# End of a two-layer streaming encoder: output rows of two token groups formed token-major from the old X and the last Y

## The chip, the cores and the metric

The kernel runs on one core of a Trainium2 chip. The metric is device time in microseconds. The engines are named as the profile names them: PE is TensorE (PEld its weight loads), DVE is VectorE, ACT is ScalarE, POOL is GpSimd, SP is SyncE. SP only issues loads and stores here.

## What is computed

One inference step of a two-layer encoder over 512 new prompt tokens and 32 sample tokens, with 1024 features each. Only the end of each layer matters here:

```python
def _rms(x, g):
    y = x32 * lax.rsqrt(jnp.mean(x32 * x32, axis=-1, keepdims=True) + EPS) * g
...
    f = jnp.square(jax.nn.relu(_rms(x, p['g_mlp_pre']) @ p['w_up'])) @ p['w_down']
    x = x + _rms(f, p['g_mlp_post'])
```

After the last layer, `x` is the output `y_prompt` (512 by 1024) and `y_sample` (32 by 1024). The norm needs the sum of squares of `f` over all 1024 features of a token before any feature of that token can be finished.

## The kernel before, in words

All activations lie feature-major in the on-chip memory: 128 features on the partitions, 8 blocks of features (k or m = 0 to 7), 544 tokens on the free axis. `X` holds x, `Y` holds f. A projection takes a weight tile of 128x1024 numbers (512 KB), which ACT splits into a high part (L1136) and DVE into a low part (L1611); PE runs three products for each of 8 blocks and two halves of the tokens.

The 544 tokens are cut in two ways. `HC` halves them: half 0 is tokens 0 to 287, half 1 is tokens 288 to 543. `cols(grp)` names five groups for the turning at the end: group 0 (the 32 sample tokens), groups 1 and 2 (prompt tokens in half 0), groups 3 and 4 (half 1, 128 tokens each).

The end of the last layer runs so:

- `down_four` and `down_end` on PE are the down projections, two output blocks m per round of four weight tiles. The last output block, m = 7, is done in two token halves (L710), half 0 first.
- DVE's `f_tile` and `f_last` add both parts of an output block in `Y` and scale it (L1921, L1925, L1711, L1718). ACT's `f_square` writes its squares and multiplies `Y` by the gain (L1219, L1220). DVE's `y_sum` adds the squares into `acc_y` (L1632).
- `y_half_sum` (L715) multiplies `acc_y` by a matrix of ones, which gives every partition the sum over the features. ACT's `y_rs_half` turns it into the inverse norm `rn` with Ln (L1161) and Exp (L1166).
- DVE's `x_chunk` runs five times for each half: `Y` times `rn` (L1643), then `X` plus `Y` (L1646). The order on DVE is half 0, with the finish of block 7 of half 1 between its chunks, then half 1.
- PE then turns each group of the new `X` to token-major in two sets of four 128x128 transposes (L1126), ACT (L1603) or for groups 3 and 4 also DVE (L2209) evicts each set of 128x512 into `y_out`, and SP stores a group once both its halves are there, in the order 0 to 4 (L521). Two of the banks are used twice, by groups that wait on an eviction.
- Beside it PE turns the last recurrent states (L1114), ACT evicts them as `last_t` (L1597), and POOL stores them in eight small transfers (L670).

The order of the work on every engine is written out by hand; semaphores hold the engines together.

Of the kernel before, what the change touches and what calls it, by code (L numbers as in the profile page):

```python
# [92 lines left out]
def hybrid_encoder(nc, A, out):  # L93
    DEPTH = A["w_in"].shape[0]
    with ExitStack() as ctx:
# [25 lines left out]
        def sem(name):  # L121
# [18 lines left out]
        neg_lam = sb("neg_lam", [P, 2])  # L140
        eps_col = sb("eps_col", [P, 1])
        warm = sb("warm", [P, 1])
        rs_tok = sb("rs_tok", [P, 5])
        mx = sb("mx", [P, 2, 4])
        neg_mx = sb("neg_mx", [P, 2, 4])
# [61 lines left out]
        lsc = at("lsc", [P, 8, KT * 2], F32, BIG + 7 * 4096 + 256)  # L207
        gain_row = at("gain_row", [KT, P], F32, BIG + 7 * 4096 + 1024)
        y_out = at("y_out", [P, 5, 2, 512], F32, BIG)
        last_t = at("last_t", [P, P], F32, BIG + 5 * 4096)  # L210


# [15 lines left out]
            sem, ("h_hi_ready", "h_lo_ready", "x_squared", "x_summed", "x_ssq", "x_rs"))  # L228
        y_squared, y_summed, y_ssq, y_rs, y_scaled, x_new = map(
            sem, ("y_squared", "y_summed", "y_ssq", "y_rs", "y_scaled", "x_new"))  # L230
        half_done, half_evacuated, first_halves_out, xsq_ready, xsq_added = map(
            sem, ("half_done", "half_evacuated", "first_halves_out", "xsq_ready", "xsq_added"))
        rs_turned, rs_tok_ready = sem("rs_turned"), sem("rs_tok_ready")
# [17 lines left out]
        relu2_done, u_hi_ready, u_lo_ready, f_scaled = map(sem, ("relu2_done", "u_hi_ready", "u_lo_ready", "f_scaled"))  # L251
        f_gained, half_trio = sem("f_gained"), sem("half_trio")
        out_turned, last_turned, last_placed, out_stored = map(sem, ("out_turned", "last_turned", "last_placed", "out_stored"))
        out_placed, out_placed_dve = sem("out_placed"), sem("out_placed_dve")
        last_stored = sem("last_stored")

        def own_wait(eng):
# [3 lines left out]

        def out_bank(grp, half):

            if grp in (1, 2):
                return PX[:, 2, :] if (grp, half) == (1, 0) else PJ[:, 1, 0, :] if (grp, half) == (1, 1) else PX[:, 3 * half, :]
            if grp == 3:
                return PX[:, 1, :] if half == 0 else PJ[:, 1, 1, :]
            return PJ[:, 0, half, :]

        def raw(n):  # L270

# [41 lines left out]
        def x_count(S):  # L313

            return 10 * (S - 1)
# [133 lines left out]
        @block.sync  # L449
        def _(sp):  # L450
            def load_x(g):

                if g == 0:
                    sp.dma_start(x_in[0:NS, 0, :], A["x_sample"][0]).then_inc(x_landed[0], 16)
                else:
                    sp.dma_start(x_in[:, g, :], A["x_prompt"][0, P * (g - 1):P * g, :]).then_inc(x_landed[g], 16)

            def load(n, source):

                sp.wait_ge(tile_done, n.value - WR + 1)  # L460
                sp.dma_start(raw(n), source).then_inc(w_landed[n.slot], 16)

            def load_early(n, source):

                need(sp, tile_done, n.value - 2 * WR + 1)
                sp.dma_start(raw(n), source).then_inc(w_landed[n.slot], 16)

            def load_apart(n, source):

                sp.dma_start(raw(n), source).then_inc(w_landed[n.slot], 16)  # L470

            def load_layer(l):

                def pair(p, first=0):
                    for j in range(first, 12):
                        load(TileNo(TL * l + 12 * p + j, j % WR), pair_source(l, p, j))

                pair(0, WR + 1)
                with sp.Fori(1, 4) as p:
                    pair(p)  # L480
                for first, name, block in ((T_GB, "w_in", 48), (T_WA, "w_branch_attn", 0), (T_WL, "w_branch_lru", 0), (T_WO, "w_out", 0)):
                    with sp.Fori(0, KT // WR) as r:
                        for j in range(WR):
                            load(TileNo(TL * l + first + WR * r + j, j), columns(name, l, block + WR * r + j))
                sp.wait_ge(lru_step, 12 * 8 * (l + 1))
                load_apart(mlp_tile(l, 0, 0, 0), columns("w_up", l, 0))
                load_early(mlp_tile(l, 0, 4, 0), columns("w_up", l, 4))
                for j in range(1, WR):
                    load(mlp_tile(l, 0, 0, j), columns("w_up", l, j))
                for j in range(1, WR):  # L490
                    load(mlp_tile(l, 0, 4, j), columns("w_up", l, 4 + j))
                for c in range(2):
                    with sp.Fori(0 if c else 2, 4) as r:
                        for j in range(WR):
                            load(mlp_tile(l, c, 4 * r, j), columns("w_up", l, 16 * c + 4 * r + j))
                    with sp.Fori(0, 4) as r:
                        for j in range(WR):
                            load(mlp_tile(l, c, 16 + 4 * r, j), down_source(l, c, j % 2, 2 * r + j // 2))


            for g in range(3):
                load_x(g)
            for i in range(WR + 1):
                load_apart(pair_tile(0, 0, i), pair_source(0, 0, i))
                if i == 1:
                    load_x(3)
                    load_x(4)
            for l in range(DEPTH):
                load_layer(l)
                if l < DEPTH - 1:  # L510
                    sp.wait_ge(x_ssq, 3 * l + 3)
                    load_apart(pair_tile(l + 1, 0, 0), pair_source(l + 1, 0, 0))
                    load_early(pair_tile(l + 1, 0, WR), pair_source(l + 1, 0, WR))
                    for i in range(1, WR):
                        load(pair_tile(l + 1, 0, i), pair_source(l + 1, 0, i))

            for g in range(5):
                sp.wait_ge(out_placed, 2 * g + 2 if g < 3 else g + 4)
                need(sp, out_placed_dve, g - 2)
                to = out["y_sample"][0] if g == 0 else out["y_prompt"][0, P * (g - 1):P * g, :]  # L520
                sp.dma_start(to, y_out[0:NS if g == 0 else P, g, :, :].rearrange("p a b -> p (a b)")).then_inc(out_stored, 16)  # L521
            sp.wait_ge(out_stored, 16 * 5)
# [152 lines left out]
        def _(pe):  # L675
# [139 lines left out]
            def gates(l, p, u):  # L815
# [6 lines left out]
                        mm = pe.matmul(PX[:, 2 * j + half, 0:LH], w_gate[:, u, j, :], uc[:, LH * half:LH * half + LH], start=True, stop=True)  # L822
                mm.then_inc(gates_done, 1)

            def sub_ssq(l, p, u):
                g2 = 2 * (4 * l + p) + u
                pe.wait_ge(o_squared, g2 + 1)
                pe.wait_ge(lru_act, 5 * g2 + 2)
                ones_sum(sq_o, 2).then_inc(o_ssq, 1)
# [179 lines left out]
            for l in range(DEPTH):  # L1009
# [89 lines left out]
                for c in range(2):  # L1099
# [4 lines left out]
                    if c == 0:  # L1104
                        pe.wait_ge(x_summed, 7 * l + 7)
                        ones_sum(acc_x).then_inc(x_ssq, 1)
                    down_four(l, c, 0)
                    with pe.Fori(1, 4 if c == 0 else 3) as r:
                        down_four(l, c, r)
                down_end(l)  # L1110

            y_half_sum(DEPTH - 1, 1, 1)
            pe.wait_ge(lru_step, 12 * 8 * DEPTH)
            pe.transpose(PX[:, 3, 0:P], last[:].rearrange("p l r k -> p (l r k)"), ident[:]).then_inc(last_turned, 1)  # L1114
            for grp in range(5):
                for half in range(2):

                    pe.wait_ge(x_new, x_count(2 * DEPTH) + 5 * (grp > 2) + 3 + 2 * half)
                    if grp == 2 and half == 1:
                        pe.wait_ge(last_placed, 1)  # L1120
                    if grp == 3 and half == 0:
                        pe.wait_ge(y_rs, 4 * 2 * DEPTH)
                    if grp == 4:
                        pe.wait_ge(out_placed, half + 1)
                    for k in range(4):
                        mm = pe.transpose(out_bank(grp, half)[:, P * k:P * k + P], X[:, 4 * half + k, cols(grp)], ident[:])  # L1126
                    mm.then_inc(out_turned, 1)
# [3 lines left out]
        def _(act):  # L1131
# [223 lines left out]
            def sub_square(l, p, u):  # L1355
# [2 lines left out]
                need(act, o_ssq, g2, first=p + u == 0)  # L1358
                act.activation(sq_o[:], O[:, 2 * p + u, :], ACT.Square).then_inc(o_squared, 1)

            def sub_log(l, p, u):
                g2 = 2 * (4 * l + p) + u
                act.wait_ge(o_ssq, g2 + 1)
# [91 lines left out]
            for l in range(DEPTH):  # L1455
# [118 lines left out]
                for c in range(2):  # L1574
# [11 lines left out]
                    else:  # L1586
                        for r in range(3):
                            down_four(l, c, r)
                down_end(l)
                if l < DEPTH - 1:  # L1590
                    renew(l, 1)
                else:
                    y_rs_half(l, 1, 0)
                    f_square(l, 7, 1)
                    y_rs_half(l, 1, 1)
            act.wait_ge(last_turned, 1)
            act.activation(last_t[:], PX[:, 3, 0:P], ACT.Copy).then_inc(last_placed, 1)  # L1597

            for grp in range(5):
                nr = NS if grp == 0 else P  # L1600
                for half in range(2 if grp < 3 else 1):
                    act.wait_ge(out_turned, 2 * grp + half + 1)
                    act.activation(y_out[0:nr, grp, half, :], out_bank(grp, half)[0:nr, :], ACT.Copy).then_inc(out_placed, 1)  # L1603

# [2 lines left out]
        def _(dve):  # L1607
# [591 lines left out]
            for c in range(5):  # L2199
# [2 lines left out]
                    f_last(DEPTH - 1, 1)  # L2202
                if c == 2:
                    y_sum(DEPTH - 1, 1, 8, HC[1])
            for c in range(5):
                x_chunk(DEPTH - 1, 1, 1, c)
            for grp in range(3, 5):
                dve.wait_ge(out_turned, 2 * grp + 2)
                dve.tensor_copy(y_out[:, grp, 1, :], out_bank(grp, 1)).then_inc(out_placed_dve, 1)  # L2209


# [27 lines left out]
```

## Time and profile before

| what | us |
|---|---|
| median of 3 runs | 2019.92 |
| lowest and highest of them | 2018.5 and 2025.07 |
| the profiled execution, its own time | 2020.43 |
| its span in the trace | 2018.6 |
| PE busy in it | 1975.9 (98%) |
| DVE busy | 1072.3 (53%) |
| ACT busy | 955.6 (47%) |

The profiled execution took 1.8 us more than its span; that part lies around the traced work. It is 0.5 us above the median of the runs. Times of trace rows are counted from the start of the span.

### The profile page before, as it was taken

To read this page: it belongs to the slowest core of one execution; us is meant where nothing else is said; L and a number is where in the kernel's file an instruction comes from. 1 tells how busy PE (TensorE), PEld (TensorE's weight loads), DVE (VectorE), ACT (ScalarE), POOL (GpSimd) and SP (SyncE) were. 2 spreads that over 40 slices of the span, in tenths; PEclk is the share of its full clock that TensorE was granted. 3 is DMA by queue.
4 is the path that set the end of the run, shared out by engine and by line. 5 is a ranking of instruction groups with operands and counts; after the bars stand their busy time and mean duration, and the time that the engine had idled before them with its cause. 6 is when DMAs were issued, how large, how long until landed. Compare 5 with 4: busy or idle time off the path is not lost.

```text
span 2018.6 us, 38666 instructions
## 1 busy us (share of the span) xinstructions
PE 1975.9 (98%) x15630; PEld 1929.2 (96%) x15630; DVE 1072.3 (53%) x1986; ACT 955.6 (47%) x1503; POOL 279.1 (14%) x306
## 2 busy tenths in 40 slices
PE   7999999999999999999989999999999999999997
PEld 7999999999998999999989999999999999999997
DVE  6657575765437432333467676767644464224334
ACT  5466666565236431342365757565732554213333
POOL 4312121100101200120041212120001012002100
PEclk9999999999999999999999999999999999999999
DMA  5323232322332323232323232322223323233331
GB/s 136 107 60 105 63 100 69 83 71 78 93 95 70 87 84 93 84 94 84 98 60 98 64 100 72 99 76 75 74 84 94 95 65 92 84 92 86 90 88 67
DMA packets 308455, 172.00 MB, mean 85 GB/s; under 512 B 7592, under 2 KB 303872, under 8 KB 308320
## 3 DMA queue, kind: packets, MB, share of 16 engines
q1 hardware_dynamic: 300768, 155.47, 27.0%
q0 software_dynamic: 7520, 14.59, 2.6%
q8 instruction: 97, 1.59, 0.3%
q14 instruction: 38, 0.31, 0.1%
q10 hardware_dynamic: 32, 0.04, 0.0%
HBM read 158.86 MB, written 11.21 MB: 84 GB/s over the span
## 4 chain that ended last, share of the span: by engine, by line
PE 81%; ACT 9%; DVE 6%; issue 3%; DMA 1%; SPq 0%; ACTq 0%; DVEq 0%
PE PJ L698 65%; PE PJ L710 3%; PE PJ L880 3%; PE PX L908 2%; ACT w_hi L1136 2%; PE PX L926 1%; DVE w_lo L1611 1%; PE PX L946 1%; DVE T L1722 1%; PE PX L962 1%; PE PX L710 1%; DMA w_raw<-in_w_in 1%; DVE uc L1855 1%; ACT L1353 1%; DVE Y L1643 1%
## 5 line engine op out<-in xcount | busy, mean ns | idle before, releaser
L1611 DVE TENSOR_TENSOR w_lo<-w_raw,w_hi 128x1024 fp32r<-128x1024 f32 x284 | 384.2, 1356 | 371.5 <-ACT w_hi L1136 370.4
L698 PE MATMUL PJ<-h_hi,w_hi 128*128 128x272 f32 x2304 | 489.9, 294 | 2.6 <-DVE T L1722 1.9
L698 PE MATMUL PJ<-h_hi,w_lo 128*128 128x272 f32 x2304 | 474.8, 288 | 0.0
L698 PE MATMUL PJ<-h_lo,w_hi 128*128 128x272 f32 x2304 | 473.8, 287 | 0.0
L1136 ACT ACTIVATE w_hi<-w_raw 128x1024 fp32r<-128x1024 f32 x284 | 297.6, 1051 | 233.4 <-DMA w_raw<-in_w_down 116.9
L698 PEld LDWEIGHTS PJ<-h_hi,w_hi 128*128 128x128 f32 x2304 | 359.3, 189 | 12.8 <-issue 9.5
L698 PEld LDWEIGHTS PJ<-h_lo,w_hi 128*128 128x128 f32 x2304 | 360.7, 188 | 0.0
L698 PEld LDWEIGHTS PJ<-h_hi,w_lo 128*128 128x128 f32 x2304 | 359.5, 189 | 0.0
L698 PE MATMUL PJ<-u_hi,w_hi 128*128 128x272 f32 x960 | 198.4, 288 | 0.0
L698 PE MATMUL PJ<-u_hi,w_lo 128*128 128x272 f32 x960 | 197.4, 288 | 0.0
L698 PE MATMUL PJ<-u_lo,w_hi 128*128 128x272 f32 x960 | 197.1, 287 | 0.0
L659 POOL TENSOR_TENSOR u_lo<-T,u_hi 128x544 f32 x64 | 87.8, 1373 | 595.6 <-ACT u_hi L1386 595.6
L698 PEld LDWEIGHTS PJ<-u_lo,w_hi 128*128 128x128 f32 x960 | 150.0, 188 | 0.0
L698 PEld LDWEIGHTS PJ<-u_hi,w_hi 128*128 128x128 f32 x960 | 149.5, 188 | 0.2
L698 PEld LDWEIGHTS PJ<-u_hi,w_lo 128*128 128x128 f32 x960 | 149.5, 188 | 0.0
L1382 ACT ACTIVATE T<-T 128x544 f32<-128x544 f32 x64 | 42.1, 658 | 205.9 <-DVE T L1908 197.1
L1286 ACT ACTIVATE s<-s,neg_mx 128x384 f32<-128x384 f32 (+4 forms) x160 | 87.8, 550 | 69.4 <-DVE neg_mx L1821 69.0
L1816 DVE CUSTOM_DVE_ANT_0 s<-PX,bias_p 128x384 f32<-128x384 f32 (+3 forms) x128 | 57.7, 488 | 62.8 <-PE PX L908 56.2
L710 PE MATMUL PJ<-h_hi,w_hi 128*128 128x288 f32 (+1 forms) x192 | 61.0, 317 | 19.6 <-DVE h_lo L1617 15.3
L880 PE MATMUL PJ<-w_hi,h_hi 128*128 128x256 f32 x256 | 75.3, 294 | 0.0
L652 POOL TENSOR_TENSOR m_lo<-GB,m_hi x16 | 21.8, 1364 | 382.5 <-ACT m_hi L1561 382.5
L1722 DVE TENSOR_TENSOR T<-PJ,rs 128x544 f32<-128x544 f32 x72 | 51.8, 720 | 39.0 <-ACT L L1320 20.8
(351 smaller groups left out, 3595.4 us busy)
## 6 DMA issues: line engine op xcount, KB each, us to landing
w_raw<-in_w_in SPq DMA_DIRECT2D x110, 512.0 KB, 3.8
w_raw<-in_w_down SPq DMA_DIRECT2D x64, 512.0 KB, 3.8
w_raw<-in_w_up SPq DMA_DIRECT2D x62, 512.0 KB, 4.1
w_raw<-in_w_branch_attn SPq DMA_DIRECT2D x16, 512.0 KB, 3.8
w_raw<-in_w_branch_lru SPq DMA_DIRECT2D x16, 512.0 KB, 3.8
w_raw<-in_w_out SPq DMA_DIRECT2D x16, 512.0 KB, 3.8
out_prompt_k<-stage POOLq DMA_DIRECT2D x16, 256.0 KB, 2.8
out_prompt_v<-GA POOLq DMA_DIRECT2D x8, 512.0 KB, 4.5
```

The lines of the kernel that those rows point to most:

```text
L652: pool.tensor_tensor(m_lo[:, i, :], GB[:, i, :], m_hi[:, i, :].bitcast(F32), ALU.subtract).then_inc(m_lo_ready, 1)
L659: pool.tensor_tensor(u_lo[:, i, :], T[:, j % 2, :], u_hi[:, i, :].bitcast(F32), ALU.subtract).then_inc(u_lo_ready, 1)
L698: mm = pe.matmul(PJ[:, buf, half, 0:HT], w[a], src[b][:, k0 + k, HT * half:HT * half + HT], start=first and k == 0 and a + b == 0, stop=en ...
L710: mm = pe.matmul(o, w[a], src[b][:, k0 + k, HC[h]], start=first and k == 0 and a + b == 0, stop=end and k == KT - 1 and a == 1)
L880: mm = pe.matmul(o, H[a][:, k, cols(grp)], w[b], start=k == 0 and a + b == 0, stop=k == KT - 1 and a == 1)
L908: mm = pe.matmul(PX[:, u, 0:kw], QK[a][R[u], m, cols(qs)], QK[b][R[u], 2 + m, NS:NS + kw], start=a + b == 0, stop=a == 1)
L1136: act.activation(w_hi[:, n.hi, :, :], raw(n), ACT.Copy).then_inc(w_hi_ready, 1)
L1286: act.activation(buf, buf, ACT.Exp, bias=neg_mx[0:nr, b, 2 * m + u:2 * m + u + 1], scale=SCALE, accum_out=lsum[0:nr, b, 2 * m + u:2 * m + ...
L1382: act.activation(T[:, j % 2, :], T[:, j % 2, :], ACT.Square).then_inc(relu2_done, 1)
L1611: dve.tensor_tensor(low(n)[:], raw(n), w_hi[:, n.hi, :, :].bitcast(F32), ALU.subtract).then_inc(w_lo_ready, 1)
L1722: dve.tensor_tensor(halves(dst), proj(n), halves(rs[:]), ALU.mult).then_inc(evacuated, 1)
L1816: dve.tensor_tensor_reduce(out=s1_at(qi, u) if m == 0 else s2_at(qi, u), in0=PX[0:nr, u, 0:w], in1=bias_s[:, u, :] if nr == NS else bias_p ...
```

## The change

For groups 3 and 4 (half 1) of the last layer's end, the new `X` is no longer formed feature-major. Instead:

- PE turns the old `X` of group 3 after round 0 of the last down projections and that of group 4 after round 2 (`turn_old_x`, two sets of four transposes each). ACT copies them into `x_tok`, token-major (`keep_old_x`). The memory is that of `T` and of the first part of the recurrent scratch.
- After the last projection PE turns the gained `Y` of both groups (`turn_y`): blocks 0 to 6 at once, block 7 when it is gained. They lie in four banks.
- `token_sums` multiplies `acc_y` of each group, as the stationary operand, with two columns of ones: one sum per token, tokens on partitions. ACT's Ln and Exp work on 128x2 numbers and give `rn_tok`.
- DVE's five `x_chunk` of half 1 and its two evictions go. Four `scalar_tensor_tensor` take their place: turned `Y` from the bank times `rn_tok`, plus `x_tok`, written into `y_out`.
- PE's turning at the very end is left for groups 0 to 2, with other banks. ACT evicts those. SP stores in the order 3, 0, 4, 1, 2.

```diff
-            return PJ[:, 0, half, :]
+            return PJ[:, 1, half, :] if grp == 0 else PX[:, half, :] if grp == 1 else PJ[:, 0, half, :]
+        def y_tok_bank(gi, half):
+            return PJ[:, 0, half, :] if gi == 0 else PX[:, 2 + half, :]
...
+            for g in (3, 0, 4, 1, 2):
+                if g < 3:
+                    sp.wait_ge(out_placed, 2 * g + 2)
+                else:
+                    sp.wait_ge(tok_out, 2 * g - 4)
...
+            def turn_old_x(gi):
+                if gi == 1:
+                    pe.wait_ge(xt_kept, 2)
+                for half in range(2):
+                    for k in range(4):
+                        mm = pe.transpose(PX[:, 2 + half, P * k:P * k + P], X[:, 4 * half + k, cols(3 + gi)], ident[:])
+                    mm.then_inc(xt_turned, 1)
+            def turn_y(ks, gained):
+                pe.wait_ge(f_gained, gained)
+                if ks[0] == 0:
+                    pe.wait_ge(evacuated, mlp_tile(DEPTH - 1, 1, 28, 0).value + 2)
+                    pe.wait_ge(xt_kept, 4)
+                for gi in range(2):
+                    for k in ks:
+                        mm = pe.transpose(y_tok_bank(gi, k // 4)[:, P * (k % 4):P * (k % 4) + P], Y[:, k, cols(3 + gi)], ident[:])
+                if ks[-1] == KT - 1:
+                    mm.then_inc(yt_turned, 1)
+            def token_sums():
+                pe.wait_ge(y_summed, sums(DEPTH - 1, 1) + 8)
+                for gi in range(2):
+                    mm = pe.matmul(PX[:, 1, 2 * gi:2 * gi + 2], acc_y[:, cols(3 + gi)], ones[:, 0:2], start=True, stop=True)
+                mm.then_inc(tok_ssq, 1)
...
                     down_four(l, c, 0)
+                    if c == 1 and l == DEPTH - 1:
+                        turn_old_x(0)
                     with pe.Fori(1, 4 if c == 0 else 3) as r:
                         down_four(l, c, r)
+                if l == DEPTH - 1:
+                    turn_old_x(1)
                 down_end(l)
 
-            y_half_sum(DEPTH - 1, 1, 1)
+            turn_y(range(0, 7), 9 * DEPTH - 2)
+            turn_y(range(7, 8), 9 * DEPTH)
+            token_sums()
             pe.wait_ge(lru_step, 12 * 8 * DEPTH)
-            pe.transpose(PX[:, 3, 0:P], last[:].rearrange("p l r k -> p (l r k)"), ident[:]).then_inc(last_turned, 1)
-            for grp in range(5):
+            pe.wait_ge(y_rs, 8 * DEPTH - 2)
+            pe.transpose(PX[:, 0, 0:P], last[:].rearrange("p l r k -> p (l r k)"), ident[:]).then_inc(last_turned, 1)
+            for grp in range(3):
                 for half in range(2):
+                    pe.wait_ge(x_new, x_count(2 * DEPTH) + 3 + 2 * half)
...
+                    if grp == 2:
+                        pe.wait_ge(tok_out, half + 1)
...
+            def keep_old_x(gi):
+                act.wait_ge(u_lo_ready, 32 * DEPTH)
+                for half in range(2):
+                    act.wait_ge(xt_turned, 2 * gi + half + 1)
+                    act.activation(x_tok[gi][:, half, :], PX[:, 2 + half, :], ACT.Copy).then_inc(xt_kept, 1)
...
                             down_four(l, c, r)
+                            if l == DEPTH - 1 and r != 1:
+                                keep_old_x(r // 2)
...
-                    y_rs_half(l, 1, 1)
+            act.wait_ge(tok_ssq, 1)
+            act.activation(rn_tok[:], PX[:, 1, 0:4].rearrange("p (g c) -> p g c", c=2)[:, :, 0], ACT.Ln,
+                           scale=1.0 / (KT * P), bias=eps_col[:, 0:1]).then_inc(tok_rs, 1)
+            act.wait_ge(tok_rs, 1)
+            act.activation(rn_tok[:], rn_tok[:], ACT.Exp, scale=-0.5).then_inc(tok_rs, 1)
...
-            for c in range(5):
-                x_chunk(DEPTH - 1, 1, 1, c)
-            for grp in range(3, 5):
-                dve.wait_ge(out_turned, 2 * grp + 2)
-                dve.tensor_copy(y_out[:, grp, 1, :], out_bank(grp, 1)).then_inc(out_placed_dve, 1)
+            dve.wait_ge(yt_turned, 1)
+            dve.wait_ge(tok_rs, 2)
+            dve.wait_ge(xt_kept, 4)
+            for gi in range(2):
+                for half in range(2):
+                    dve.scalar_tensor_tensor(out=y_out[:, 3 + gi, half, :], in0=y_tok_bank(gi, half), scalar=rn_tok[:, gi:gi + 1],
+                                             in1=x_tok[gi][:, half, :], op0=ALU.mult, op1=ALU.add).then_inc(tok_out, 1)
```

## Rows read from the trace of the kernel before

**Rows 1.** Windows: busy us per engine, granted clock, DMA share, GB/s; down projections.
```profile
1903.00:1927.00 24.00, 24.00 (x195) 24.00 (x194) 7.61 (x8) 6.64 (x8) 1.36 (x1) 1.00 0.30 88
```
**Rows 2.** Chain that ended last, in order: start us, us, what; the end.
```profile
1986.71 8.49 PE PJ L710 x66
...
2012.88 0.69 DVE y_out L2209
```
**Rows 3.** Timeline of PE (start us, us, engine, line, op); the end.
```profile
1986.55 0.29 PE L710 MATMUL PJ<-u_hi,w_hi 128*128 128x288 f32 x1
...
1999.08 0.28 PE L710 MATMUL PJ<-u_hi,w_lo 128*128 128x256 f32 x1
2002.61 0.70 PE L715 MATMUL PX<-acc_y,ones 128*128 128x256 f32 x2 [3.24 <-DVE acc_y L1632]
2006.44 1.06 PE L1126 MATMUL PX<-ident,X 128*128 128x128 f32 x4
2007.29 1.06 PE L1126 MATMUL PJ<-ident,X 128*128 128x128 f32 x4
```
**Rows 4.** Timeline of PE in layer 1's attention: transposes inside the product stream.
```profile
1187.37 0.66 PE L926 MATMUL PX<-ident,s 128*128 128x128 f32 x4
1187.78 0.50 PE L698 MATMUL PJ<-h_hi,w_hi 128*128 128x272 f32 x2
1188.12 0.41 PE L698 MATMUL PJ<-h_lo,w_hi 128*128 128x272 f32 x2
```
**Rows 5.** Timeline of DVE; last low weight parts, then the end.
```profile
1978.66 2.44 DVE L1611 TENSOR_TENSOR w_lo<-w_raw,w_hi 128x1024 fp32r<-128x1024 f32 x2 [1.68 <-ACT w_hi L1136]
...
2002.13 0.42 DVE L1632 TENSOR_TENSOR acc_y<-acc_y,sq 128x256 f32<-128x256 f32 x1
2004.72 0.76 DVE L1646 TENSOR_TENSOR X<-X,Y 128x576 f32<-128x576 f32 x1
...
2007.90 0.69 DVE L1646 TENSOR_TENSOR X<-X,Y 128x512 f32<-128x512 f32 x1
2008.51 0.69 DVE L1643 TENSOR_TENSOR Y<-Y,rn 128x512 f32<-128x512 f32 x1
...
2010.56 0.69 DVE L1646 TENSOR_TENSOR X<-X,Y 128x512 f32<-128x512 f32 x1
```
**Rows 6.** Timeline of ACT; last weight splits, then the end.
```profile
1977.59 1.04 ACT L1136 ACTIVATE w_hi<-w_raw 128x1024 fp32r<-128x1024 f32 x1
1981.16 0.20 ACT L1140 ACTIVATE warm<-eps_col 128x1 f32<-128x1 f32 x1
2001.11 0.49 ACT L1220 ACTIVATE Y<-Y,par 128x256 f32<-128x256 f32 x1
2001.62 1.28 ACT L1161 ACT_TABLE_LOAD   x1
2008.39 0.60 ACT L1603 ACTIVATE y_out<-PJ 128x512 f32<-128x512 f32 x1 [0.26 <-PE PJ L1126]
2010.09 0.60 ACT L1603 ACTIVATE y_out<-PX 128x512 f32<-128x512 f32 x1 [0.26 <-PE PX L1126]
```
**Rows 7.** Groups by shape, DVE: count, busy us, mean ns, idle before.
```profile
L2168 DVE SCALAR_TENSOR_TENSOR GB<-GB,PJ 128x544 f32 x16 | 11.5, 721 | 20.4 <-PE PJ L698 20.4
```
**Rows 8.** Windows of half a microsecond at the end, columns as in Rows 1.
```profile
2010.00:2010.50 0.50, 0.50 (x5) 0.50 (x3) 0.50 (x1) 0.41 (x1) 0.42 (x1) 0.50 1.04 385
2010.50:2011.00 0.50, 0.31 (x2) 0.01 (x1) 0.47 (x2) 0.35 (x2) 0.00 (x0) 0.93 1.03 402
...
2014.00:2014.50 0.50, 0.00 (x0) 0.00 (x0) 0.00 (x0) 0.00 (x0) 0.00 (x0) 1.00 1.01 401
...
2016.00:2016.50 0.50, 0.00 (x0) 0.00 (x0) 0.00 (x0) 0.00 (x0) 0.00 (x0) 1.00 0.39 148
```
**Rows 9.** Timeline of SP's issues, then the issue table (KB each, us to landing).
```profile
2013.67 0.33 SPq L521 DMA_DIRECT2D out_y_prompt<-y_out  x1
...
out_y_prompt<-y_out SPq DMA_DIRECT2D x4, 512.0 KB, 2.7
```

More of the change, by code:

```diff
@@ L142, in hybrid_encoder @@
         warm = sb("warm", [P, 1])
+        rn_tok = sb("rn_tok", [P, 2])
         rs_tok = sb("rs_tok", [P, 5])
@@ L209, in hybrid_encoder @@
         y_out = at("y_out", [P, 5, 2, 512], F32, BIG)
+        x_tok = (T[:].rearrange("p a b -> p (a b)")[:, 0:1024].rearrange("p (a b) -> p a b", b=512), at("x_tok4", [P, 2, 512], F32, R_AT)[:])
         last_t = at("last_t", [P, P], F32, BIG + 5 * 4096)
@@ L230, in hybrid_encoder @@
             sem, ("y_squared", "y_summed", "y_ssq", "y_rs", "y_scaled", "x_new"))
+        xt_turned, xt_kept, yt_turned, tok_ssq, tok_rs, tok_out = map(
+            sem, ("xt_turned", "xt_kept", "yt_turned", "tok_ssq", "tok_rs", "tok_out"))
         half_done, half_evacuated, first_halves_out, xsq_ready, xsq_added = map(
@@ L253, in hybrid_encoder @@
         out_turned, last_turned, last_placed, out_stored = map(sem, ("out_turned", "last_turned", "last_placed", "out_stored"))
-        out_placed, out_placed_dve = sem("out_placed"), sem("out_placed_dve")
+        out_placed = sem("out_placed")
         last_stored = sem("last_stored")
@@ L262, in out_bank @@
         def out_bank(grp, half):
[L264 to L267, printed above, removed]
-            return PJ[:, 0, half, :]
+            return PJ[:, 1, half, :] if grp == 0 else PX[:, half, :] if grp == 1 else PJ[:, 0, half, :]
+        def y_tok_bank(gi, half):
+            return PJ[:, 0, half, :] if gi == 0 else PX[:, 2 + half, :]
         def raw(n):
@@ L515, in _ @@
                         load(pair_tile(l + 1, 0, i), pair_source(l + 1, 0, i))
-            for g in range(5):
-                sp.wait_ge(out_placed, 2 * g + 2 if g < 3 else g + 4)
-                need(sp, out_placed_dve, g - 2)
+            for g in (3, 0, 4, 1, 2):
[3 more added lines that the diff above has]
+                    sp.wait_ge(tok_out, 2 * g - 4)
                 to = out["y_sample"][0] if g == 0 else out["y_prompt"][0, P * (g - 1):P * g, :]
@@ L1107, in _ @@
                     down_four(l, c, 0)
+                    if c == 1 and l == DEPTH - 1:
+                        turn_old_x(0)
                     with pe.Fori(1, 4 if c == 0 else 3) as r:
                         down_four(l, c, r)
+                if l == DEPTH - 1:
+                    turn_old_x(1)
                 down_end(l)
-            y_half_sum(DEPTH - 1, 1, 1)
+            turn_y(range(0, 7), 9 * DEPTH - 2)
+            turn_y(range(7, 8), 9 * DEPTH)
+            token_sums()
             pe.wait_ge(lru_step, 12 * 8 * DEPTH)
-            pe.transpose(PX[:, 3, 0:P], last[:].rearrange("p l r k -> p (l r k)"), ident[:]).then_inc(last_turned, 1)
-            for grp in range(5):
+            pe.wait_ge(y_rs, 8 * DEPTH - 2)
+            pe.transpose(PX[:, 0, 0:P], last[:].rearrange("p l r k -> p (l r k)"), ident[:]).then_inc(last_turned, 1)
+            for grp in range(3):
                 for half in range(2):
-                    pe.wait_ge(x_new, x_count(2 * DEPTH) + 5 * (grp > 2) + 3 + 2 * half)
-                    if grp == 2 and half == 1:
+                    pe.wait_ge(x_new, x_count(2 * DEPTH) + 3 + 2 * half)
+                    if grp == 0:
+                        pe.wait_ge(evacuated, TL * DEPTH)
+                    if grp == 1 and half == 0:
                         pe.wait_ge(last_placed, 1)
[L1121 to L1124, printed above, removed]
+                    if grp == 1 and half == 1:
+                        pe.wait_ge(tok_rs, 1)
+                    if grp == 2:
+                        pe.wait_ge(tok_out, half + 1)
                     for k in range(4):
@@ L1594, in _ @@
                     f_square(l, 7, 1)
-                    y_rs_half(l, 1, 1)
+            act.wait_ge(tok_ssq, 1)
[3 more added lines that the diff above has]
+            act.activation(rn_tok[:], rn_tok[:], ACT.Exp, scale=-0.5).then_inc(tok_rs, 1)
             act.wait_ge(last_turned, 1)
-            act.activation(last_t[:], PX[:, 3, 0:P], ACT.Copy).then_inc(last_placed, 1)
-            for grp in range(5):
+            act.activation(last_t[:], PX[:, 0, 0:P], ACT.Copy).then_inc(last_placed, 1)
+            for grp in range(3):
                 nr = NS if grp == 0 else P
-                for half in range(2 if grp < 3 else 1):
+                for half in range(2):
                     act.wait_ge(out_turned, 2 * grp + half + 1)
@@ L2204, in _ @@
                     y_sum(DEPTH - 1, 1, 8, HC[1])
-            for c in range(5):
-                x_chunk(DEPTH - 1, 1, 1, c)
-            for grp in range(3, 5):
-                dve.wait_ge(out_turned, 2 * grp + 2)
-                dve.tensor_copy(y_out[:, grp, 1, :], out_bank(grp, 1)).then_inc(out_placed_dve, 1)
+            dve.wait_ge(yt_turned, 1)
+            dve.wait_ge(tok_rs, 2)
+            dve.wait_ge(xt_kept, 4)
+            for gi in range(2):
+                for half in range(2):
+                    dve.scalar_tensor_tensor(out=y_out[:, 3 + gi, half, :], in0=y_tok_bank(gi, half), scalar=rn_tok[:, gi:gi + 1],
+                                             in1=x_tok[gi][:, half, :], op0=ALU.mult, op1=ALU.add).then_inc(tok_out, 1)
 _INS = ["x_prompt", "x_sample", "cache_k", "cache_v", "state_conv", "state_lru", "w_in", "lambda_q1", "lambda_k1", "lambda_q2",
```

## Prediction

> **What bounds the kernel now.** I read the busy shares first (PE 98% of the span), then the windows over the last down projections, then the chain that ended last, then each engine's timeline at the end. In the windows PE is busy 24.00 us of 24.00 at a granted clock of 1.00, while DVE and ACT are busy under 9 us and DMA has a share of 0.3 [rows 1]. So anything added to PE's stream there moves the end by its full length. The chain confirms it: it runs along PE's products up to the last block [rows 2]. I call the end of the last projection product E: 1999.08 + 0.28 = 1999.36 [rows 3]. All later times are given as E plus something.
>
> Behind E the span runs another 19.2 us (2018.6 - 1999.4), and PE no longer bounds it. DVE finishes half 0 at 2004.72 + 0.76 = 2005.48, E+6.1. It then works on half 1 up to 2011.25 (ten operations), PE turns the last three sets, and DVE evicts the last at 2013.57, E+14.2 [rows 2, 5]. The last store is issued at 2013.67 and lands 2.7 us later, at about 2016.4; the rest up to 2018.6 is the end of the program [rows 9]. The reader should see one more thing: the last two stores run back to back. In the windows the bytes move at 401 GB/s, so 512 KB takes 524 KB / 401 = 1.31 us, and the movement ends in the window from 2016.0, after 0.39 of its half microsecond, at 2016.2, which is E+16.8 [rows 8]. That is the number to beat.
>
> **The change, part by part.**
>
> *Added before E: 16 transposes of old X and 4 copies on ACT.* Four transposes inside the product stream, at the full clock, take from 1187.37 to 1187.78, 0.41 us or 0.103 each; the pair of products behind them shows 0.50 [rows 4], where a pair in steady flow shows 0.41, so each insertion costs some 0.09 more. Two insertions of eight: 16 x 0.103 + 2 x 0.09 = 1.8; I take 1.9 us. PE has no idle time there to hide it. The lower bound is 1.6 (no seam), the upper is the price at half clock, from 2006.44 to 2007.29 for four, 0.21 each [rows 3], which gives 3.4. A gain is excluded, because nothing is taken out of this stretch. PE's wait for the first two copies comes some 24 us after their cause and holds nothing.
>
> *The copies on ACT* are nearest to the evictions of 128x512 at 0.60 [rows 6], so 1.2 us per group. Queued behind them are the splits of the next two weight tiles, and behind those DVE's low parts and PE. Before, the first of the last pair is split from 1977.59 [rows 6], and both low parts are done by 1978.66 + 2.44 = 1981.1 [rows 5]; PE starts on that pair at 1986.55 [rows 3]. Over 5 us of slack cover 1.2: nothing. If the cover were gone, each copy would cost PE its 0.6.
>
> *Removed behind E:* `y_half_sum` of half 1, Ln and Exp over 256 columns, five `x_chunk` (2011.25 - 2005.48 = 5.8 us of DVE), 16 transposes of new X, two evictions on ACT and two on DVE.
>
> *Turning Y.* 14 transposes start right at E, since their Y was gained before: 14 x 0.103 = 1.5 us, E+1.6. Block 7 is gained at 2001.11 + 0.49 = 2001.60, E+2.24 [rows 6]; its two transposes are done by E+2.6. The queue behind them waits anyway for `acc_y`, which DVE finishes at 2002.55, E+3.2 [rows 5]. So the turning is free unless PE runs slower.
>
> *Token sums.* No row shows a product with two columns. Above, two of them cost twice the pair of L715 with 256 columns, 2 x 0.70 = 1.4 [rows 3]; below, no less than the 0.28 of one product. I take 0.6, as so few columns lie nearer to the lower end: E+3.8. A gain is excluded, as ACT must wait for it.
>
> *The inverse norm.* The table load for Ln stands ahead of the wait already now (2001.62 [rows 6], while the sum comes at 2003.3 [rows 3]) and stays hidden. The one for Exp, 1.28 us, stays exposed. A tiny ACT operation takes 0.20 [rows 6]. So 3.8 + 0.05 + 0.20 + 1.30 + 0.20 = E+5.6. DVE is busy with half 0 until E+6.1 in either kernel, so the norm is ready 0.5 us before it is wanted.
>
> *Four fused operations.* The nearest row is the same instruction with one operand in a PJ bank, 721 ns for 544 columns [rows 7], so 0.69 for 512; independent operations start 0.61 apart (2007.90 to 2008.51) [rows 5]. From E+6.15: group 3 is placed at E+7.45, group 4 at E+8.7. The bounds are 0.61 and 0.79 apiece; they move group 3 by 0.3 us at most.
>
> *Groups 0 to 2.* The second set of group 0 still waits for the end of half 0, E+6.1, and five sets follow, as before. At half clock they come 0.85 apart and group 2 is placed at 2010.69, E+11.3, as now; group 1 at 2008.99, E+9.6 [rows 6]. At the full clock ACT's 0.60 apiece rules, E+9.9 and E+8.7. Groups 0 to 2 no longer wait for half 1 behind them; the reuse of group 3's banks by group 2 needs fused operations done at E+6.8 and E+7.5, before PE wants them.
>
> *Stores.* SP's new order is 3, 0, 4, 1, 2. A store begins to move about 0.75 us after its issue (2013.67 + 2.7 - 1.31 leaves 1.4 us for both ends, and I give half to each). Group 3 moves from E+8.3; group 0 is a quarter of the size, 0.33. With 4 x 1.31 + 0.33 = 5.6 us of bytes the chain ends at E+13.9, no matter whether group 2 is issued at E+10 or at E+11.4. POOL's small stores fall among them; I add 0.2: E+14.1. That no store stands idle behind an earlier one in SP's queue is part of this: group 0 is placed at about E+7.5, group 1 by the time group 4 moves.
>
> *The sum.* Behind E: 14.1 - 16.8 = -2.7 us. Before E: +1.9. Together -0.8 us. Against the profiled execution this is 2020.43 - 0.8 = 2019.6, with a span of 2017.8; that execution lies 0.5 above the median of the runs, so for the median I say 2019.92 - 0.8 = 2019.1.
>
> **A rule weighed against the trace.** Between 2003.3 and 2010.6 PE ran nothing but 128x128 transposes, and in that stretch the granted clock rose: 0.50 in the window from 2010.0, 0.93 in the next [rows 8]. The Trainium skill, "TensorE: Matmul & The Clock Gate", Part 4: PE-mode transpose, says that transposes do not count as work that engages the full clock. By that rule the clock would fall soon after E and stay low. This trace speaks against it.
>
> **The rivals.**
>
> *The clock is at 1.2 GHz (0.50) from E on.* For it: PE's work behind E is thin and broken, and the clock did fall before the sets of group 0's second half now. Against it: the rise above, and more PE work right behind E than now. Price: Y's 14 transposes at 0.21 take 3.0, block 7 ends at E+3.4, the sums come 0.7 later, DVE starts at E+6.35. Stores end at E+14.3. In all -0.6: 2019.3. It decides nothing large.
>
> *The stores do not pack.* If every store leaves a gap, or if POOL's eight small ones cost 0.8 rather than 0.2, the chain ends at E+14.9 and the sum is 0.0: 2019.9.
>
> *Slower: the norm comes late.* The place is ACT behind the token sums. If the table for Ln is also loaded behind the wait (+1.3) and the token sums take their upper price (+0.8), the norm is ready at E+7.7, the fused operations start 1.55 late and the stores end at E+15.7. With the insertions at 2.4 the sum is +1.3: 2021.2. It decides from a norm at about E+7.0, where -1.8 behind E no longer pays for 1.9 before it. Against it: the order of load and wait in today's rows.
>
> *More than forecast.* Seams at nothing (1.6), stores from E+8.1 with POOL's small ones in their gaps, E+13.7: -1.5, 2018.4.
>
> **How the numbers follow.** Chances: forecast 0.50, low clock 0.15, no packing 0.15, late norm 0.12, more 0.08. The terms alone span 2018.4 to 2021.2. The runs of before span 2018.5 to 2025.07 themselves, so a median of a few runs may lie a microsecond or two off either way; the range is 2016.8 to 2022.3. A measurement can tell about 0.3% (6 us) from no change. No case reaches 6 us on either side: it would take the whole stretch behind E cut by half, or PE held for 6 us more. Faster by over 0.3%: 0.03; within: 0.93; slower: 0.04.
>
> **What the profile after would show.** Right: PE without a gap up to E, E later by about 1.9; the pair of weight splits 1.2 later with PE not waiting; the first fused operation at E+6.1 with DVE not idle before it; Exp done before that; four fused operations at 0.6 to 0.7; DMA share near 1 from E+8.3 to E+14; span 2017.8. Wrong: PE idle on the low parts of a weight tile behind an insertion; a table load behind the token sums; a DMA share with gaps between stores; E later by over 2.5.

## The result and the profile after

The changed kernel is slower: 2032.92 us median (2031.03 to 2035.35, 4 runs) against 2020.2 for the kernel before (2018.5 to 2025.07). The ratio is 1.0054, 95% interval 1.0036 to 1.0071. Forecast were 2019.1 us and a range up to 2022.3, so the result lies 10.6 us outside. The profiled execution took 2035.35 us with a span of 2033.5, 14.9 more than the span of before. One later run, of the kernel with only h moved, took 2411.26 us at a mean granted clock of 0.75 and is left out of its figures.

Read E, the end of the last projection product, first: it answers to [rows 3]. This is PE's timeline at the end of the changed kernel (start us, us, engine, line, op).

```profile
2012.71 0.28 PE L716 MATMUL PJ<-u_hi,w_lo 128*128 128x256 f32 x1
2012.84 0.93 PE L848 MATMUL PJ<-ident,Y 128*128 128x128 f32 x7
2013.60 0.93 PE L848 MATMUL PX<-ident,Y 128*128 128x128 f32 x7
...
2016.22 0.61 PE L856 MATMUL PX<-ones,acc_y 128*128 128x2 f32 x4 [0.51 <-DVE acc_y L1688]
```

E is now 2012.99, 13.6 us later than 1999.36. I had expected 1.9. Behind E the span runs another 20.5 us, where it ran 19.2 before; I had expected 2.7 less. Of the sum, the part before E was +13.6 for +1.9 and the part behind it +1.2 for -2.7. Both failed, and not only by their size. Yet the new pieces behaved nearly as costed. The insertions of old X, in the chain that ended last (start us, us, what):

```profile
1899.91 38.47 PE PJ L704 x307
1938.38 0.87 PE PX L837 x8
1939.26 48.12 PE PJ L704 x384
1987.38 0.87 PE PX L837 x8
1988.25 12.03 PE PJ L704 x96
```

Each costs 0.87 us, 1.74 together. What has changed is the neighbour: 96 products, one pair of weight tiles, take 12.03 us, 125.3 ns each. The chain of before has 124.4 ns each over the same stage:

```profile
1959.96 26.75 PE PJ L698 x215
```

The windows show the same of a stretch that the change doesn't touch. These are the windows from 830 to 900 us and from 925 to 995 us, up and down projections of the first layer, columns as in [rows 1]; first the kernel before, then the changed one.

```profile
830.00:900.00 70.00, 70.00 (x565) 70.00 (x564) 29.16 (x24) 25.64 (x35) 16.07 (x12) 1.00 0.31 87
925.00:995.00 70.00, 70.00 (x565) 70.00 (x564) 26.19 (x34) 21.56 (x27) 0.00 (x0) 1.00 0.33 95
```
```profile
830.00:900.00 70.00, 70.00 (x561) 70.00 (x561) 27.47 (x23) 27.19 (x36) 15.72 (x12) 1.00 0.33 90
925.00:995.00 70.00, 70.00 (x561) 70.00 (x560) 26.17 (x35) 22.30 (x27) 0.00 (x0) 1.00 0.33 93
```

In 70 us at the full granted clock, PE is busy throughout in both and starts 561 products where it started 565. From one start to the next that is 125.3 ns against 124.4, taken from the starts in the trace. Busy time, share and clock give nothing away; only the count does. Over the 14,000 steady products of the span (gaps of 110 to 140 ns from start to start) the mean went from 123.87 to 124.58 ns. Put side by side one by one, the 13,931 that are steady in both traces took 10.2 us more in sum. The insertions are 1.74. The granted clock fell to 0.50 in six stretches before E here, in four before, and the products in them cost 2.3 us more than there. What is left of the 13.6 us is -0.6, from single waits.

The end, by the timelines of ACT, DVE and SP in the changed kernel:

```profile
2015.24 1.28 ACT L1648 ACT_TABLE_LOAD   x1
2016.87 0.26 ACT L1648 ACTIVATE rn_tok<-PX,eps_col 128x2 f32<-128x2 f32 x1 [0.34 <-PE PX L856]
2017.14 1.28 ACT L1651 ACT_TABLE_LOAD   x1
2018.44 0.20 ACT L1651 ACTIVATE rn_tok<-rn_tok 128x2 f32<-128x2 f32 x1
...
2023.71 0.60 ACT L1659 ACTIVATE y_out<-PJ 128x512 f32<-128x512 f32 x1 [0.26 <-PE PJ L1169]
```
```profile
2018.33 0.76 DVE L1702 TENSOR_TENSOR X<-X,Y 128x576 f32<-128x576 f32 x1
2019.01 1.40 DVE L2266 SCALAR_TENSOR_TENSOR y_out<-PJ,rn_tok,T 128x512 f32<-128x512 f32 x2
2020.33 1.40 DVE L2266 SCALAR_TENSOR_TENSOR y_out<-PX,rn_tok,x_tok 128x512 f32<-128x512 f32 x2
```
```profile
2020.43 0.36 SPq L527 DMA_DIRECT2D out_y_prompt<-y_out  x1
2020.91 0.37 SPq L527 DMA_DIRECT2D out_y_sample<-y_out  x1
2021.75 2.91 SPq L527 DMA_DIRECT2D out_y_prompt<-y_out  x3
```

The norm is ready at E+5.65 (forecast 5.6), the fused operations run from E+6.0 to E+8.7, ACT is done at E+11.3. And the windows of one microsecond show that the bytes stop at 2027.5, E+14.5 (forecast 14.1):

```profile
2026.00:2027.00 1.00, 0.00 (x0) 0.00 (x0) 0.00 (x0) 0.00 (x0) 0.00 (x0) 0.50 1.01 398
2027.00:2028.00 1.00, 0.00 (x0) 0.00 (x0) 0.00 (x0) 0.00 (x0) 0.00 (x0) 0.50 0.53 209
2028.00:2029.00 1.00, 0.00 (x0) 0.00 (x0) 0.00 (x0) 0.00 (x0) 0.00 (x0) 0.50 0.00 0
...
2032.00:2033.50 1.50, 0.00 (x0) 0.00 (x0) 0.00 (x0) 0.00 (x0) 0.00 (x0) 0.50 0.00 0
```

Then nothing is busy for 6 us. In [rows 8] and [rows 9] that silence was 2.4 us, and I had put it down to "the end of the program". It has an owner. The trace's records of waits and drains, which the views leave out as not busy, say (start us, ns, engine, instruction), first before, then after:

```
2012.37   38 GpSimd COMPARE_BRANCH      (its stores have landed)
2012.52 5865 GpSimd DRAIN
2016.72   38 Sync   COMPARE_BRANCH      (the last large store has landed)
2018.43   17 GpSimd EVENT_SEMAPHORE     (lets all engines end)
...
2027.22   38 GpSimd COMPARE_BRANCH
2027.37 5865 GpSimd DRAIN
2028.27   38 Sync   COMPARE_BRANCH
2033.28   17 GpSimd EVENT_SEMAPHORE
```

In both kernels the end was set by POOL: its eight small stores of the recurrent states land, and then a drain of 5.87 us runs before all engines may end. Before, that drain ended 1.7 us behind the last large store; now it begins at E+14.4 instead of E+13.2. So the large stores did land 2.1 us earlier (E+15.3 against E+17.4), and this was worth nothing. The last small one was issued 0.5 us earlier (E+10.0 against E+10.5) and yet landed 1.2 later (E+14.2 against E+13.0). More of the large ones now move at the same time: the DMA share was 1.06 and 0.76 in the microseconds from E+9 and E+10, where it was 0.4 and 0.6 before. That this is the reason is argued, not tested.

### The profile page after: what moved, and what is told of

It reads as the page before. It is cut to its first block, busy times and chain, and to the rows that moved or that the text cites. A ratio compares the mean times of both kernels' runs of the same rounds, so it can differ in the third digit from the quotient of the medians.

```text
span 2033.5 us, 38700 instructions
## 1 busy us (share of the span) xinstructions
PE 1991.3 (98%) x15648; PEld 1945.1 (96%) x15648; DVE 1067.9 (53%) x1978; ACT 955.7 (47%) x1505; POOL 278.7 (14%) x306
## 4 chain that ended last, share of the span: by engine, by line
PE 88%; ACT 6%; DVE 3%; issue 2%; DMA 1%; SPq 0%; ACTq 0%; DVEq 0%
PE PJ L704 69%; PE PJ L914 4%; PE PJ L716 4%; PE PX L942 2%; PE PX L960 1%; PE PX L828 1%; PE PX L980 1%; PE PX L996 1%; PE PX L716 1%; ACT w_hi L1179 1%; DMA x_in<-in_x_prompt 1%; PE PX L818 1%; DVE T L1778 1%; DVE Y L1699 0%; PE PX L875 0%
## 5 line engine op out<-in xcount | busy, mean ns | idle before, releaser
L704 PEld LDWEIGHTS PJ<-h_hi,w_hi 128*128 128x128 f32 x2304 | 363.4, 189 | 12.7 <-issue 9.4
L716 PE MATMUL PJ<-h_hi,w_hi 128*128 128x288 f32 (+1 forms) x192 | 61.9, 323 | 19.9 <-DVE h_lo L1673 15.3
```

The lines of the kernel that those rows point to most:

```text
L704: mm = pe.matmul(PJ[:, buf, half, 0:HT], w[a], src[b][:, k0 + k, HT * half:HT * half + HT], start=first and k == 0 and a + b == 0, stop=en ...
L716: mm = pe.matmul(o, w[a], src[b][:, k0 + k, HC[h]], start=first and k == 0 and a + b == 0, stop=end and k == KT - 1 and a == 1)
```

## The experiments

Two theories for the front. *Places*: `rn_tok` is declared in the middle of the list of tiles, and the running offset puts everything behind it (`rs`, `T`, `h_hi`, `h_lo`, `u_hi`, `u_lo`, `Y` and more) 32 bytes higher; that slows the products. *Not places*: chip, clock or the new instructions. The ratios are those on record; they are not the quotients of the two medians. For the end: the *drain* theory against something else that keeps the end.

**The changed kernel with the old places.**

```diff
-        rn_tok = sb("rn_tok", [P, 2])
         rs_tok = sb("rs_tok", [P, 5])
...
         R_AT = room(7 * 552 * 4)
+        rn_tok = sb("rn_tok", [P, 2])
```

> The changed kernel, with rn_tok declared behind all other tiles, so that every tile lies where it lay before the change. Theory A: the time falls from 2033 by 8 to 10 us to about 2024; what is left over the kernel before is +1.7 for the 16 transposes of old X and about +1.2 at the end, where POOL's last drain (5.87 us) starts after its eight small stores have landed, 1.2 us later behind the last product than before. Theory B: 2033 stays, or falls without regard to the places.

Measured: 2023.51 us median (10 runs) against 2022.48 of the kernel before, ratio 1.0007 (0.9998 to 1.0017). E at 1998.60, the end 20.5 behind it. (E is 0.8 earlier than before in spite of the insertions: only two stretches at a granted clock of 0.50 lie ahead of it, against four.) Product spacing 124.4 ns in all four up and down stages of a layer. One declaration moved took away nearly the whole loss.

**The changed kernel again, and the kernel before with the changed places**, on one chip:

> The changed kernel once more, unaltered, on one chip with the three below and the kernel before. If the 12 us over the kernel before belong to the places of the tiles and not to a chip: ratio 1.005 again, 125.3 ns from product to product in the steady stream of the projections (124.4 in the kernel before and in the changed kernel with the old places).

```diff
+        unused = sb("unused", [P, 2])
         rs_tok = sb("rs_tok", [P, 5])
```

> The kernel before, with an unused tile of 8 bytes (32 with rounding) declared where the changed kernel has rn_tok: every tile lies where the changed kernel has it, and nothing else is changed. Places theory: 125.3 ns per product instead of 124.4, over some 13,000 products of the steady stream 8 to 11 us, so 2030 to 2033. If instead the instructions or waits of the change slow the stream: no difference from the kernel before.

Measured: the changed kernel 2035.92, ratio 1.0073 (1.0047 to 1.0098), 125.3 ns. The kernel before with 32 unused bytes 2030.3, ratio 1.0044 (1.0027 to 1.0060), 125.3 ns. Its window of the up projections, columns as above:

```profile
830.00:900.00 70.00, 70.00 (x561) 70.00 (x560) 28.42 (x23) 26.72 (x36) 16.33 (x12) 1.00 0.33 90
```

561 products again, with not one instruction of the change in it. (The window from 925 us, whose end reaches into the last output block of its stage, has 562 here and 563 in the changed kernel with the old places; by the starts the spacing in that stage is 125.3 and 124.4 ns.) The places theory holds. They alone cost 2023.84 x 0.0044 = 8.9 us, with the interval 5.5 to 12.1; the two medians (2023.84 for the kernel before on this chip) differ by 6.5, and E in the trace is 9.5 later than before.

**Which places.** The kernel before, with h moved and u not, or the other way round. In the first, `warm` (32 bytes) is declared between the areas of h and u, so h lies 32 bytes lower, and so do `rs`, `T` and the small tiles in front of it. In the second an unused tile there puts u and all behind it, `Y` among them, 32 bytes higher.

```diff
-        warm = sb("warm", [P, 1])
...
         H_AT = room(2 * KT * TILE)
+        warm = sb("warm", [P, 1])      # first kernel
+        unused = sb("unused", [P, 2])  # second kernel, warm left alone
         BIG = room(4 * KT * TILE)
```

> The kernel before, with warm declared between h_hi/h_lo and the area of u_hi/u_lo: rs, T and h_hi/h_lo lie 32 bytes lower, u_hi/u_lo and all behind them where they were. Theory A: the products that stream h (input and up projections, about two thirds of all) are slower, those that stream u (down projections) keep 11.95 us per pair; the time is about 2025. Theory B: 2020. If it isn't the streamed operand but another of the shifted tiles, the pair of down tiles or the total tells: all of the 8 us or none.

> The kernel before, with an unused 8-byte tile declared between h_hi/h_lo and the area of u_hi/u_lo: h lies in its old place, u and all behind it 32 bytes higher, where the changed kernel has it. If the spacing follows the place of the tile that is streamed: up projections (stream h) 124.4 ns per product, down projections (stream u) 125.3. If it follows any other tile: the same in both. In the counterpart, with h moved by 32 bytes and u not, the down projections kept 124.4 and the others did not.

The windows of the first kernel (up projections, which stream h, then down projections, which stream u), then of the second:

```profile
830.00:900.00 70.00, 70.00 (x562) 70.00 (x561) 29.12 (x24) 25.32 (x35) 15.84 (x12) 1.00 0.31 86
925.00:995.00 70.00, 70.00 (x565) 70.00 (x564) 25.83 (x34) 21.01 (x25) 0.00 (x0) 1.00 0.34 96
```
```profile
830.00:900.00 70.00, 70.00 (x565) 70.00 (x564) 29.13 (x24) 25.66 (x35) 15.75 (x12) 1.00 0.31 86
925.00:995.00 70.00, 70.00 (x561) 70.00 (x560) 26.07 (x33) 21.48 (x26) 0.00 (x0) 1.00 0.33 94
```

With h moved, the stage that streams h loses (562; 125.0 ns) and the one that streams u keeps 565. With u moved it is the other way round (565 and 561; 124.4 and 125.3 ns). Weights, banks and instructions are the same. The tiles that DVE, ACT and POOL write have moved too (`T`, `Y`), so the traffic of these engines is a rival. The traces speak against it. In the kernel with 32 unused bytes, successive weight tiles of the second down stage found the other three engines busy for 98, 7, 98 and 3% of the time, and the mean spacing over the 48 products of each was 125.3 ns all the same; with the old places it was 124.4 ns at 10, 92, 12 and 93%. PE's own operands are left, and of these only the streamed tile had moved. The first kernel took 2028.65 us (7 runs), ratio 1.0026 (1.0014 to 1.0037), more than the 2025 I gave it. Its first set of up projections ran at 126.1 ns, and so did the merge stages whose operand's high part lies in the moved area. The second kernel was run once, at 2027.2; there the merge stages whose low part alone had moved kept 124.4.

**What about the place.** The kernel before with everything behind the small tiles 32 and 64 bytes lower:

```diff
-        warm = sb("warm", [P, 1])
-        lsum = sb("lsum", [P, 2, 4])   # only in the second
...
         R_AT = room(7 * 552 * 4)
+        warm = sb("warm", [P, 1])
+        lsum = sb("lsum", [P, 2, 4])   # only in the second
```

> The kernel before, with only the place of one small tile changed: warm (32 bytes per partition) is declared behind all others, so that rs, T, h_hi/h_lo, u_hi/u_lo and all behind them lie 32 bytes lower. Between the two traces each pair of down-projection tiles took 11.95 us before and 12.03 after, from the first layer on. Theory A (the 32 bytes that rn_tok put in front of these tiles slow the products): the pair takes 12.03 here too and the time rises by 7 to 9 us, to about 2028. Theory B (another chip, or stretches at low granted clock that fall where they like): no difference, 2020 within 1 us.

> The kernel before, with two small tiles (warm, lsum) declared behind all others: the same tiles now lie 64 bytes lower. Theory A1 (what counts is the address modulo 64, relative to the weights): 11.95 us per pair and 2020 again. Theory A2 (a shift as such, or a finer alignment, counts): anything between 2020 and 2030. Theory B (chip, clock): 2020.

Both expectations fell. 32 bytes lower: 2025.54, ratio 1.0010 (0.9997 to 1.0023). The first set of up projections of each layer ran at 126.1 ns, the other up and down projections at 124.4. 64 bytes lower, where a rule modulo 64 wanted no change: 2037.07, ratio 1.0069 (1.0053 to 1.0086), 125.6 ns in every stage, the slowest of all. Moreover, h lies in the same place in the 32-byte kernel and in the h-only kernel, and the second set of up projections ran at 124.4 ns in the one and at 125.0 in the other. Each stage settles in one spacing and keeps it to its end, within 0.02 ns from weight tile to weight tile; which one depends on the place, but not on the streamed tile's address alone. Even one and the same kernel shows this: in the changed kernel run again the merge stages of the first layer ran at 125.0 ns and those of the second at 125.3, where both had 125.3 in its first trace. What decides it stays open.

**The end.** The recurrent states are final long before the last projections. In these kernels they are turned, evicted and stored after round 0 of them; the changed kernel has the old places here.

```diff
-        last_t = at("last_t", [P, P], F32, BIG + 5 * 4096)
+        last_t = at("last_t", [P, P], F32, S_AT + 14080)
...
                     down_four(l, c, 0)
                     if c == 1 and l == DEPTH - 1:
                         turn_old_x(0)
+                        pe.wait_ge(lru_step, 12 * 8 * DEPTH)
+                        pe.transpose(PX[:, 1, 0:P], last[:].rearrange("p l r k -> p (l r k)"), ident[:]).then_inc(last_turned, 1)
...
+                            if l == DEPTH - 1 and r == 0:
+                                act.wait_ge(last_turned, 1)
+                                act.activation(last_t[:], PX[:, 1, 0:P], ACT.Copy).then_inc(last_placed, 1)
```

> The changed kernel with the old places, and the recurrent states turned, evicted and stored after round 0 of the last down projections, not at the very end (last_t lies in another scratch area). Drain theory: the end is set by POOL, whose last instruction, a drain of 5.87 us, begins when its eight small stores have landed (14.2 us behind the last product in the changed kernel, 13.0 in the kernel before). With the small stores gone from the end, the span ends with the last large store, 15 to 15.6 us behind the last product in place of 20.5: 4.9 us less than the changed kernel with the old places, ratio to the kernel before 0.998. Rival: the drain waits for something else (it comes out as long, or as late), and nothing is gained.

> The same move of the recurrent states in the kernel before. Drain theory: the last large store lands 17.4 us behind the last product and the span ends some 0.4 us later, 17.8 in place of 19.2: 1.4 us less than the kernel before, ratio 0.9993. Rival: no change. The difference between this and the changed kernel with the same move is then what the change is worth by itself: 1.7 us more in front of the last product, 2.3 less behind it.

Measured: the changed kernel 2019.52, ratio 0.9992 (0.9978 to 1.0006); the kernel before 2022.39, ratio 0.9995 (0.9981 to 1.0008). In the trace of the first, E is 2000.20 and the span ends at 2015.5, 15.3 behind it in place of 20.5; in the second 18.2 in place of 19.2, and 17.8 when run again. POOL's last issue and SP's, changed kernel:

```profile
1934.19 0.52 POOL L676 DMA_DIRECT2D out_sample_lru<-last_t  x1
```
```profile
2007.66 0.36 SPq L527 DMA_DIRECT2D out_y_prompt<-y_out  x1
2008.13 0.37 SPq L527 DMA_DIRECT2D out_y_sample<-y_out  x1
2008.98 2.36 SPq L527 DMA_DIRECT2D out_y_prompt<-y_out  x3
```

The last large store lands at 2015.11 and the span ends 0.4 us later. The drain theory holds for the end. Since the medians couldn't tell so little, both were run again in five rounds:

> The changed kernel with the old places and the early store of the recurrent states, again, in more rounds, next to the kernel before. The sum of the traces: 1.7 us more in front of the last product and 3.7 less behind it (15.5 in place of 19.2), so 2.0 us less, ratio 0.999. Whether it can be told from no change: runs of one kernel spread over several us, as stretches at half the granted clock fall in a different number of places, 1.7 us for each, so the interval will be about 0.1% wide.

> The kernel before with the early store alone, again, in more rounds: 1.5 us less than the kernel before, ratio 0.9993; the changed kernel with the same move 0.3 to 0.6 us less than this one, which the rounds will hardly tell.

Changed kernel, old places, early store: 2021.0 against 2021.98, ratio 0.9990 (0.9980 to 0.9999). Kernel before with the early store: 2021.48, ratio 0.9996 (0.9987 to 1.0005). The first is faster than the kernel before by an interval that just stays clear of 1; in its earlier runs it did not (0.9978 to 1.0006). That it beats the second isn't shown; the traces alone put it ahead (15.3 and 15.2 us behind E against 18.2 and 17.8, for 1.74 more before it).

## Why the prediction was wrong

- **"Added before E: 1.9 us."** The 16 transposes cost 1.74, so this term was right. The step that failed is the one before it: that only what is added to PE's stream moves E. A line of the diff that I never costed, the declaration of `rn_tok`, was put at nothing and cost about 10 us: 10.2 by the steady products of the traces, 8.9 by the ratio of the places alone. The two ratios of the changed kernel against its version with the old places, 1.0054 and 1.0073 against 1.0007, give 9.5 and 13.4. No row of before prices it, but the diff shows that the tile is inserted ahead of all streamed operands in a list with a running offset. Another 2.3 us of the 13.6 are stretches at the low clock, whose number differs from one execution to the next; that part is chance.
- **"The rest up to 2018.6 is the end of the program."** This was wrong as a reading, and it hid the bound. I followed the last busy thing and took the silence behind it as a constant. It was POOL's drain, 5.87 us, started when the last small store had landed. The drain already ended 1.5 us after SP was done (2018.38 against 2016.87), so landing the large stores earlier could win nothing, and the small stores themselves landed 1.2 us later (E+14.2 against E+13.0), which is the whole of the longer end. The term -2.7 was the way of the large stores, and these set the end in neither kernel.
- **Turning Y, token sums, norm, fused operations, evictions** came as forecast: 14 transposes in 1.7 us with the block 7 pair behind them, norm at E+5.65, ACT done at E+11.3, the pair of splits with no wait of PE. The four fused operations took 0.74 each for 0.69, and started 0.66 apart, inside their bounds.
- **Stores:** the bytes ended at E+14.5 for 14.1, the last landed 2.1 us earlier than before. Right in mechanism, a little short in size, with no effect on the end.
- **The rivals:** "The clock is at 0.50 from E on" did not come as stated. The granted clock was still 1.00 while Y was turned, fell at 2018.2 (E+5.2) and then stayed at 0.50 to the end; it moved no term of the sum. By the rule of the Trainium skill that was weighed ("TensorE: Matmul & The Clock Gate", Part 4: PE-mode transpose) transposes don't bring the full clock. In this trace it stayed at 0.50 through 4.5 us of transposes up to 2023.7, which agrees. Two other traces with the same instructions at the end speak against the rule, as the kernel before does: the clock rose again at 2022.4 in the changed kernel run again, and at 2007.6 with the old places, each with nothing but transposes on PE since the fall. What decides it stays open. Late norm did not occur. Of the stores that don't pack there was half: the DMA share fell to 0.76 in the window from 2023.0, among 1.03 to 1.06, and the bytes ended midway between the forecast (E+14.1) and this rival (E+14.9). The slower side was the right one for reasons that no rival named.
- **Range and chances:** 0.04 on slower by over 0.3% was too small because the cases came only from the terms that I had costed. A measured ratio of 1.0054 lies above that bound.

## What to carry to other kernels

Read a diff's declarations like its instructions: a small new tile in front of large streamed ones moves them all, and the products can get slower by 0.7% in stages that nobody touched; declare it last, and compare the number of products in equal windows, since busy share and clock don't show it. When the end of a span is silent, ask which engine's last instruction ends it, and store early what is final early, above all from the engine whose drain is longest. A tail shortened by 2 us is only worth what the next chain behind it allows.

## What the runs showed of the hardware

- The start-to-start time of products of 128x128 by 272 columns at the full granted clock was 124.4, 125.0, 125.3, 125.6 or 126.1 ns, with the tiles moved by 32 or 64 bytes. Averaged over the 48 products of a weight tile it didn't vary by more than 0.02 ns within a steady stage, whether the other engines were busy or not.
- GpSimd's drain at the end took 5865 ns in all 13 traces, and it began after its own stores had landed. The other drains took 1.3 to 3.1 us (PE), 0.7 to 2.9 (DVE) and 0.6 to 0.7 (ACT), and ended before the last large store had landed.
- The small stores of GpSimd took longer to land in the changed kernel, where more of the large ones move beside them: the issue table's medians for the recurrent states of 4 KB went from 2.4 and 2.2 us before to 3.7 and 3.6 us after.
- The granted clock fell to 0.50 in one to six stretches before E, in different places for one and the same kernel (six and four in two traces of the changed kernel). It accounts for a part of the spread of 3 to 10 us between runs of one kernel: over the 21 to 23 runs of the kernel before on each of three chips, span and mean granted clock go together (correlation -0.77, -0.60 and -0.52). How large a part was not tested.
